# Sharing the residual additions of a normed branch between GpSimd and VectorE in a two-layer GLA and mixture-of-experts kernel

## What is computed

```python
def rmsnorm(x, g):
    xf = x.astype(jnp.float32)
    y = xf * lax.rsqrt(jnp.mean(xf * xf, axis=-1, keepdims=True) + EPS)
    return (y * g.astype(jnp.float32)).astype(x.dtype)
...
        x = x + gt1 * rmsnorm(y_x, g_mix_post[i])
...
        x = x + gt2 * rmsnorm(ffn(modulate(rmsnorm(x, g_ffn_pre[i]), sh2, sc2)), g_ffn_post[i])
```

## Time and profile before

| | |
|---|---|
| Median of 3 runs | 1743.89 us (1742.58 to 1746.1) |
| Span of the profiled execution, first to last instruction | 1737.8 us |
| The profiled execution's own time | not given apart; the median stands 6.1 us over its span |
| PE busy | 1638.6 us (94%) |
| DVE busy | 955.3 us (55%) |
| ACT busy | 536.7 us (31%) |
| POOL busy | 4.0 us, 13 instructions |
| DMA, mean | 274 GB/s; some 410 GB/s in most of the second half |

### The profile page before, as it was taken

One profiled execution on the slowest core, in us unless ns is written; L12 is line 12 of the kernel. 1 busy time (PEld: TensorE's weight loads), 2 busy tenths in 40 slices (PEclk: granted clock), 3 DMA queues, 4 the chain that ended last, 5 costly groups with the idle time before them and its releaser, 6 DMA issues.

```text
span 1737.8 us, 21264 instructions
## 1 busy us (share of the span) xinstructions
PE 1638.6 (94%) x8432; PEld 1123.6 (65%) x8432; DVE 955.3 (55%) x1343; ACT 536.7 (31%) x682; POOL 4.0 (0%) x13
## 2 busy tenths in 40 slices
PE   6999999999999999998999999999989999888886
PEld 3788666788888885797788834887338873333322
DVE  4588775544445776699598712986129951110102
ACT  4421243400000005414577502774027730000001
POOL 0000000000000000000000000000000000000000
PEclk9999999999999999999999999999999999999999
DMA  9320785333321316327599999999999999999996
GB/s 360 136 97 1 283 299 189 102 97 97 97 97 37 133 58 236 102 94 291 216 411 372 353 384 408 412 408 411 415 407 412 409 410 411 407 412 409 411 414 265
DMA packets 160619, 476.26 MB, mean 274 GB/s; under 512 B 10002, under 2 KB 33012, under 8 KB 146164
## 3 DMA queue, kind: packets, MB, share of 16 engines
q1 hardware_dynamic: 158688, 474.24, 71.1%
q10 hardware_dynamic: 1812, 0.41, 0.1%
HBM read 473.58 MB, written 1.05 MB: 273 GB/s over the span
## 4 chain that ended last, share of the span: by engine, by line
PE 72%; SPq 14%; DVE 5%; DMA 5%; issue 3%; ACT 2%; ACTq 0%; DVEq 0%; POOL 0%; POOLq 0%
SPq L785 11%; PE ps L918 10%; PE ps L920 10%; PE ps L919 10%; PE ps L1376 7%; PE ps L1368 6%; PE ps L1370 6%; PE ps L1276 6%; SPq L789 3%; PE ps L1316 2%; PE ps L882 2%; PE ps L841 2%; DMA ring<-in_e_w 1%; DMA work<-in_e_w 1%; DMA ring<-in_w_in 1%
## 5 line engine op out<-in xcount | busy, mean ns | idle before, releaser
L1276 PE MATMUL ps<-ring,work 128*64 128x512 f32 x960 | 223.5, 614 | 32.8 <-DMA ring<-in_e_w 30.3
L2534 DVE TENSOR_TENSOR norms<-work,ps 64x256 f32<-64x256 f32 x70 | 29.7, 424 | 324.5 <-ACT work L1839 323.0
L918 PE MATMUL ps<-ring_rounded 128*128 128x512 f32 (+1 forms) x536 | 190.6, 356 | 2.9 <-DVE norms L2316 1.6
L1276 PEld LDWEIGHTS ps<-ring,work 128*64 128x64 f32 x960 | 73.7, 141 | 169.7 <-issue 166.7
L1978 DVE TENSOR_TENSOR ring_rounded<-ring,hT_rounded 128x2048 fp32r<-128x2048 f32 x72 | 163.0, 2287 | 16.9 <-ACT hT_rounded L1862 16.8
L920 PE MATMUL ps<-ring_rounded 128*128 128x512 f32 (+1 forms) x472 | 163.3, 346 | 0.0
L1862 ACT CAST hT_rounded<-ring 128x2048 fp32r<-128x2048 f32 x72 | 136.6, 1914 | 33.3 <-PE ps L1370 18.7
L920 PE MATMUL ps<-mixT_rounded,ring_rounded 128*128 128x512 f32 x328 | 127.6, 389 | 0.0
L918 PE MATMUL ps<-mixT_rounded,work_rounded 128*128 128x512 f32 x304 | 118.3, 389 | 0.0
L919 PE MATMUL ps<-hT_rounded,work_rounded 128*128 128x512 f32 x304 | 118.3, 389 | 0.0
L918 PEld LDWEIGHTS ps<-ring_rounded 128*128 128x128 f32 x536 | 101.3, 189 | 19.5 <-issue 2.4
(11 more groups left out here) (307 smaller groups left out, 2866.5 us busy)
## 6 DMA issues: line engine op xcount, KB each, us to landing
ring<-in_e_w SPq DMA_DIRECT2D x288, 1024.0 KB, 18.4
ring<-in_w_mod SPq DMA_DIRECT2D x24, 2048.0 KB, 11.0
ring<-in_w_in SPq DMA_DIRECT2D x12, 2048.0 KB, 8.9
mixT<-in_e_w SPq DMA_DIRECT2D x24, 1024.0 KB, 18.5
work<-in_e_w SPq DMA_DIRECT2D x24, 1024.0 KB, 18.6
ring<-in_w SPq DMA_DIRECT2D x22, 1024.0 KB, 7.8
ring<-in_w_out SPq DMA_DIRECT2D x4, 2048.0 KB, 15.2
ring<-in_w SPq DMA_DIRECT2D x4, 2048.0 KB, 7.7
```

What stands on the lines that cost most here:

```text
L918: pe.matmul(acc, w_high_, x_high_, start=first, stop=False)
L1276: ins = pe.matmul(narrow_bank(b)[H * w:H * w + H, :], xsel[:, k, 0:H], piece_words(e, pair[w])[:, at_:at_ + BLK], start=(k == 0), stop=(k ...
```

## The change

GpSimd gets the additions of rows 1, 3, 5 and 7 in each of the three branches. VectorE keeps all multiplications and the additions of rows 0, 2, 4 and 6, and its order is new: rows 1 and 0 are multiplied first, then rows k+3 and k+2 before the addition of row k. A second semaphore counts the odd additions, and ScalarE's squares wait for the one or the other.

```diff
@@ semaphores
+        odd_res_ready = sem("odd_res_ready")
@@ gpsimd
+            def add_odd_rows(post, c0):
+
+                for k in range(1, KD, 2):
+                    pool.wait_ge(scaled, KD * (2 * post + 1) + k)
+                    pool.tensor_tensor(xT[:, k, c0:], xT[:, k, c0:], hT[:, k, c0:], ALU.add).then_inc(odd_res_ready, 1)
+
+            add_odd_rows(0, 0)
+            add_odd_rows(1, 0)
+
             wait_drained(pool, ("y", DEPTH - 1, 0))
             pool.iota(iota_s, pattern=[[1, 256]], base=0, channel_multiplier=0).then_inc(iota2_done, 1)
             pool.iota(iota_b, pattern=[[1, P]], base=0, channel_multiplier=-1).then_inc(iota2_done, 1)
             pool.iota(iota_e, pattern=[[1, NE], [-1, NE]], base=0, channel_multiplier=0).then_inc(iota2_done, 1)
             pool.memset(yacc, 0.0).then_inc(sums_clear, 1)
+            add_odd_rows(2, CTX)
@@ scalar, the squares of layer 1's entry, and those after each mixer
-                        act.wait_ge(res_ready, (2 * L - 1) * KD + k + 1)
+                        act.wait_ge(odd_res_ready if k % 2 else res_ready, (2 * L - 1) * KD // 2 + k // 2 + 1)
...
-                    act.wait_ge(res_ready, 2 * L * KD + k + 1)
+                    act.wait_ge(odd_res_ready if k % 2 else res_ready, L * KD + k // 2 + 1)
@@ vector, add_branch
+                scale(1)
                 scale(0)
-                for k in range(KD):
-                    if k + 1 < KD:
-                        scale(k + 1)
-                    dve.wait_ge(scaled, KD * (2 * post + 1) + k + 1)
+                for k in range(0, KD, 2):
+                    if k + 3 < KD:
+                        scale(k + 3)
+                        scale(k + 2)
+                    dve.wait_ge(scaled, KD * (2 * post + 1) + k + 2)
                     dve.tensor_tensor(xT[:, k, c0:], xT[:, k, c0:], hT[:, k, c0:], ALU.add).then_inc(res_ready, 1)
```

## The result

The changed kernel takes 1748.11 us (median of 5 runs, 1746.55 to 1749.44), the kernel before beside it 1742.58 us (1739.52 to 1746.1). The ratio is 1.0034 with a 95% interval of 1.0021 to 1.0047: slower by some 6 us.

A forecast was written before the change was run, and what follows sets the result against it. The prediction took TensorE as the bound, with VectorE's additions nearly off the chain. Delays of 4.8, 3.4 and 0.3 us at post 0, 1 and 2 made 8.5 us, added to 1743.9 for 1752.4 us; range 1743.4 to 1758.5 us.

The forecast's parts named there:

- the 0.05 us at post 0: At post 0, row 6's square was the one released by a residual addition, which cost 0.05 us.
- My reading against the chain there: At post 2, row 2's square at 851.77 waits for row 0's buffer, not VectorE; its addition is 2.9 us early.
- Turn by turn: At all three places VectorE and GpSimd block each other for whole instructions; 8.5 us slower, 1747.5 to 1758.2 us; chance 0.55.
- side by side: Rival at all three places: engines don't block each other, nothing is late; 1743.8 us, 0.05 us gained; chance 0.22.
- VectorE first: Rival: GpSimd gets in only after VectorE's back-to-back series, 7.2 us at post 0; 8.4 us together, 1752.3 us; chance 0.14.
- The lower clock: Rival: idle at post 0 or post 1 lowers the next stretch's clock to 0.72; about 3 us more; chance 0.06.
- announced signs: Timeline marks: GpSimd additions 1.0 to 1.4 us, post 0 series 12 to 13 us, chain through VectorE and GpSimd.
- the price of a GpSimd turn: For 512 columns at post 0 and post 1: 1.16 us per GpSimd addition, plus 0.09 us at each hand-over.
- the 0.3 us of the sum: At post 2, row 4's addition ends at 853.33 against its square at 853.04, so 0.3 us late.
- The products behind the gate's diagonals: At post 2, line 1183's products start 0.7 us later, with 0.48 us of idle behind them, adding nothing beyond 0.3 us.
- Row 4 as the one that decides: Row 4's late addition sets the delay: 4.8 us at post 0, 3.4 us at post 1.
- Passing the delay on: Between the places TensorE is what others wait for, so all 8.5 us of delay reach the end.

The follow-up runs named there:

- run 1: All sixteen operations on VectorE in the changed kernel's order, nothing on GpSimd; ratio to the kernel before 1.0002 (0.9993 to 1.0011).
- run 8: GpSimd adds only rows 1 and 3, VectorE the other six, each straight behind its pair; 1741.09 us, the kernel before beside it 1741.76 us.
- run 4: Kernel before plus four GpSimd additions of two constants into unused words at post 0 and post 1; 1748.53 us, kernel before 1740.73 us.
- run 6: Kernel before plus four GpSimd copies of 128x512, one read and one write, at post 0 and post 1; 1745.13 us, kernel before 1741.76 us.
- run 5: Kernel before plus four GpSimd MEMSETs of 128x512, which read nothing, at post 0 and post 1; 1742.67 us, kernel before 1741.76 us.
- run 7: Kernel before plus GpSimd constant additions beside VectorE's PSUM copies, beside added SBUF copies and with VectorE nearly idle; 1746.79 us, kernel before 1741.76 us.
- run 2: Changed kernel, but VectorE adds each even row straight behind the multiplications of its pair; ratio to the kernel before 1.0025 (1.0015 to 1.0035).
- run 10: GpSimd adds all eight rows at each place, VectorE only multiplies, in row order; ratio to the kernel before 1.0028 (1.0019 to 1.0038).

## Why the prediction was right

**The bound and the removed work.** That TensorE's square sum, not VectorE, set the end of each place was right, but for the 0.05 us at post 0. At post 1 the distance stayed at 13.19 and 13.20 us with another order (run 1) and with a series 1.2 us longer (run 8). At post 2, where VectorE's series got 0.8 us longer (6.2 us for 5.4), it stayed at 9.32 us. My reading against the chain there is shown by the wait of 0.68 us that stayed when VectorE's operations moved.

**Turn by turn.** The likeliest case, at 0.55, is what happened. No row of before showed it; it was a choice between two ends, and the runs show that it was the right one: two reads block for 1.07 us (run 4), one for 0.41 us (run 6), an instruction without reads does not block (run 5), and an operation out of PSUM isn't blocked (run 7). The Trainium skill (SBUF — State Buffer, SBUF: two separate sides) states an exclusive lock on a shared port pair between GpSimd and VectorE, held for the whole instruction. The trace agrees that one stands still, with 1.75 us for 0.69, and that a MEMSET beside VectorE operations with two SBUF inputs cost nothing. It differs in the length: VectorE was shut out for 1.07 us by an addition of 1.26 us and more.

The rival side by side falls with the first of these rows. The rival VectorE first, which would have given the same time to 0.1 us, falls by the trace and not by the time: GpSimd got its turn behind the operation in progress each time; its first addition is through at 292.1, 2.4 us into VectorE's series, and not after its end. The lower clock didn't come where the rival had it: behind the start of post 0 and of post 1 the granted clock is 1.00 over 32 us, in both kernels. The dip behind post 2 is there in both kernels. In the two traces it is deeper in the changed one (0.57 for 0.72 over 12 us, with TensorE busy for 10.0 and 10.1 of them; mean of the span 0.986 for 0.989), but the stretch behind post 2 is only 0.49 us longer in all.

Three of the announced signs missed. GpSimd's records are 1.65 us, not 1.0 to 1.4, because they hold a wait; VectorE's series ended 11.6 us after its start, not 12 to 13; and the chain goes through VectorE alone there, not through GpSimd. The others came: operations lengthened by more than 1 us beside each GpSimd addition, the square of row 4 released by VectorE and 3.85 us late against VectorE's start, post 2 as it was.

**The term that was mis-sized** is the price of a GpSimd turn. I had 1.16 us from the middle of two bounds, and 0.09 us for each of two hand-overs, 1.34 us in all. It measured 1.07 us. Both parts were off, in opposite ways: the addition alone is longer (1.26 us and more), but VectorE is shut out for 1.07 us of it only, hand-overs included. With 1.07 us my own series gives row 4 at 11 x 0.60 + 4 x 1.07 = 10.9 us; its square started at 11.04 (300.70 less 289.66). I had 11.96. Those 0.9 to 1.1 us are the difference at post 0 (3.79 for 4.8 us) and at post 1 (2.45 for 3.4 us). At post 2 a turn is 0.54 us (1.97 less 1.43) where I had 0.58 + 0.16: row 4 comes at 11 x 0.34 + 4 x 0.54 = 5.9 us, and its square starts at 6.4 (853.04 less 846.63), so the 0.3 us of the sum measured 0. The products behind the gate's diagonals, which I had 0.7 us late, start 9.12 us after VectorE's first operation, for 9.11 us before. The sum is 6.2 us for 8.5, and the runs say 5.9.

**The base of the sum.** The forecast of 1752.4 us is 4.3 us above the measured 1748.11. The turns are 2.3 us of this. Another 1.3 us is the base: I added to 1743.9 us, the median of three runs, and the kernel before measured beside the changed one at 1742.58 us. The remaining 0.7 us are within the runs' spread. The 6.1 us between median and span were not a fixed offset either: the profiled execution of the changed kernel takes 1.8 us more than its span.

**Row 4 as the one that decides** was right, and run 2 puts a number on it: with as many turns but each even addition straight behind its pair, 2.2 us of the 6.2 go away. What remains, 4.0 us, is the turns and what is left of the order. **Passing the delay on** was right as well: the stretch from the Ln of post 0 to VectorE's start at post 1 is 370.34 us before and 370.35 us after.

## What to carry to other kernels

Before work goes from VectorE to GpSimd, ask what VectorE does meanwhile. While it read two SBUF tensors here, an addition of 512 fp32 columns on GpSimd shut it out for 1.07 us, more than the 0.60 us in which it would do the addition itself. A copy within SBUF was held up too (0.95 us, seen once). GpSimd cost VectorE nothing with work that only writes (run 5), and beside copies out of PSUM (run 7). And where the consumers take rows in order, look at the row that the new order puts last before its consumer, not at the sum of busy time.

## What was not expected

GpSimd's turn is shorter than its instruction: unhindered, the addition takes 1.26 us and more, but only 1.07 us of it keep VectorE out, and of a copy of 0.93 to 1.02 us only 0.41 us (those records may hold some waiting). Why the turn is the shorter one, no run shows. A single-input VectorE copy from SBUF to SBUF is blocked like an operation with two inputs (1.375 us for 0.427).

Doubling GpSimd's share changed next to nothing. Ahead of run 10 this was forecast (6.7 us), but it goes against the simple view that the loss grows with the number of additions. Each further turn takes 1.07 us and gives back only 0.60 us, and yet the loss is 6.1 us for 6.2. The rows come in the order in which the squares take them, and run 2 put 2.2 us on the order.
